# Attention levels of the mixing blocks placed between the streamed projections, S5 directly behind them, products by halves on GpSimd

## The reference, cut to what matters

```python
u, q, k, v, g_out, a_low = jnp.split(h @ w_in[layer], IN_SPLITS, axis=-1)
y_s5 = _s5_group(u, ...)          # 32 groups of 64 complex states, recurrence over the tokens
y_gla = _gla_group(q, k, v, g_out, a_low, w_alpha_up, b_alpha, head_gain)
y = jnp.concatenate([y_s5, y_gla], axis=-1) @ w_out[layer]
```

## Time and profile before

| | us |
|---|---|
| timed runs, median of 3 | 2970.05 |
| the profiled execution | 2976.95 |
| its span, first to last instruction | 2975.2 |
| TensorE busy | 2657.4 |
| VectorE busy | 2241.1 |
| ScalarE busy | 1465.4 |
| GpSimd busy | 941.0 |
| mean granted TensorE clock | 0.925 of full |

### The profile page before, as it was taken

How to read it: one execution, slowest core, us unless ns; L and a number is a source line. 1 busy time by engine, 2 the same in 40 slices (tenths; PEclk the granted TensorE clock), 3 DMA queues, 4 the chain that set the end, 5 groups by cost and what they waited for, 6 DMA issues and landing times. The chain is left out here.

```text
span 2975.2 us, 47277 instructions
## 1 busy us (share of the span) xinstructions
PE 2657.4 (89%) x17674; PEld 2414.6 (81%) x17674; DVE 2241.1 (75%) x2501; ACT 1465.4 (49%) x1886; POOL 941.0 (32%) x568
## 2 busy tenths in 40 slices
PE   7998689999998897568997756799999999999997
PEld 7998489999988887348997633699999999999986
DVE  6676566766767755877777677589888888988888
ACT  4343443433444334114333311477777777777765
POOL 6970059788408301324999142000000000000000
PEclk9999599999999998689998858899999999999999
DMA  8764067677444453025773301499999999999986
GB/s 292 250 209 149 22 226 248 217 248 253 168 186 156 162 176 131 25 68 208 255 241 114 131 22 54 164 344 344 336 346 344 341 345 331 342 343 341 344 311 228
DMA packets 129207, 670.56 MB, mean 225 GB/s; under 512 B 14672, under 2 KB 14992, under 8 KB 80064
## 3 DMA queue, kind: packets, MB, share of 16 engines
q1 hardware_dynamic: 111024, 604.72, 55.6%
q0 software_dynamic: 18064, 64.21, 6.3%
HBM read 667.82 MB, written 1.05 MB: 225 GB/s over the span
## 5 line engine op out<-in xcount | busy, mean ns | idle before, releaser
L1595 PE MATMUL work<-xT_hi,wh_gu 128*128 128x256 f32 x2120 | 611.2, 288 | 57.1 <-DVE xT_lo L871 25.2
L1596 PE MATMUL work<-xT_lo,wh_gu 128*128 128x256 f32 x2120 | 608.7, 287 | 0.0
L1597 PE MATMUL work<-xT_hi,wl_gu 128*128 128x256 f32 x2120 | 608.0, 287 | 0.0
L1595 PE MATMUL work<-wh_gu,mixT_hi 128*128 128x256 f32 x1792 | 513.0, 286 | 4.7 <-DVE mixT_lo L1317 3.2
L1596 PE MATMUL work<-wl_gu,mixT_hi 128*128 128x256 f32 x1792 | 505.7, 282 | 0.0
L1597 PE MATMUL work<-wh_gu,mixT_lo 128*128 128x256 f32 x1792 | 505.4, 282 | 0.0
L754 DVE TENSOR_TENSOR wl_gu<-raw_gu,wh_gu 128x2048 fp32r<-128x2048 f32 x158 | 390.2, 2469 | 124.3 <-ACT wh_gu L378 123.8
L1595 PEld LDWEIGHTS work<-xT_hi,wh_gu 128*128 128x128 f32 x2120 | 415.7, 196 | 68.5 <-issue 39.7
L1596 PEld LDWEIGHTS work<-xT_lo,wh_gu 128*128 128x128 f32 x2120 | 416.4, 196 | 4.8
L1597 PEld LDWEIGHTS work<-xT_hi,wl_gu 128*128 128x128 f32 x2120 | 415.5, 196 | 0.0
L1595 PE MATMUL acc<-wh_d,h_hi 128*128 128x512 f32 x912 | 379.6, 416 | 4.5 <-DVE wl_d L1329 2.7
(11 more groups left out here) (438 smaller groups left out, 4873.8 us busy)
## 6 DMA issues: line engine op xcount, KB each, us to landing
raw_gu<-in_w_gu SPq DMA_DIRECT2D x271, 1024.0 KB, 4.9
raw_d<-in_w_d SPq DMA_DIRECT2D x269, 512.0 KB, 5.4
scratch<-in_w_gu SPq DMA_DIRECT2D x112, 1024.0 KB, 7.2
scratch<-in_w_d SPq DMA_DIRECT2D x112, 512.0 KB, 7.8
scratch<-in_w_mod POOLq DMA_DIRECT2D x96, 512.0 KB, 3.7
scratch<-in_s_b POOLq DMA_DIRECT2D x16, 256.0 KB, 2.9
rows<-in_norm_post POOLq DMA_DIRECT2D x6, 512.0 KB, 4.4
rows<-in_ln_g POOLq DMA_DIRECT2D x4, 512.0 KB, 4.0
```

Source lines behind the costliest of these rows:

```text
L1595: pe.matmul(out_, w[0], m[0], start=start, stop=False)
L1596: pe.matmul(out_, w[0], m[1], start=False, stop=False)
L1597: return pe.matmul(out_, w[1], m[0], start=False, stop=stop)
```

## The change

- TensorE: the alpha product stands behind unit U+1, the identity set behind the first part of U+2, and levels 0 to 7 behind the parts of units U+3 to U+5 (`stream` with `behind`). Behind them come the first S5 product, the products with v, the second S5 product, and the transposes, which now go to the banks 0 and 1 of `work`.
- ScalarE: it evacuates the q, k, alpha, v and u blocks, and applies Silu straight from PSUM.
- VectorE: it makes `CS` behind the low part of U+2, takes the low parts of U+4 to U+6 behind masks 0, 3 and 6, puts each level into `SC` with `copy_predicated` from PSUM instead of a product and a sum, and scales, gains and gates the heads inside round 0 of S5 with one instruction for a head and token tile; the low parts of the heads go into round 1.
- GpSimd: a level multiplies the left half of each pair of stretches with keys and the right half with queries, in place, in the buffer of the decays, which serves as both operands of the scores. It multiplies the gate by the head gain, and loads `CRAW` ahead of the levels.

The core of the diff:

```diff
@@ TensorE, mix2
-                unit(U, [T, T, T])
-                unit(U + 1, [T, T, v[0]])
-                unit(U + 2, v[1:4])
-                unit(U + 3, go[0:3])
-                unit(U + 4, [go[3], T, T])
-                unit(U + 5, [T, None, T])
-                pe.wait_ge(t_evac, TSTART[b + 1])
-                pe.wait_ge(alphaw_in, 16 * (n + 1))
...
+                def level(j):
+
+                    if j < 0:
+                        pair_scores(QG, KG, 0).then_inc(g["scores"], 1)
+                        return
+                    pe.wait_ge(g["decayed"], 8 * n + j + 1)
+                    x = DF[j % 3]
                     if j:
                         pe.wait_ge(g["masked"], 9 * n + j)
-                        pair_scores(QS[j % 2], KS[j % 2], (j + 1) % 2).then_inc(g["scores"], 1)
-                        continue
+                        pair_scores(x, x, (j + 1) % 2).then_inc(g["scores"], 1)
+                        return
+                    pe.wait_ge(g["zabs"], n + 1)
...
+                t_, u_ = [t_block(i) for i in range(5)], [u_block(i) for i in range(4)]
+                stream(U, t_[0:3])
+                stream(U + 1, [t_[3], t_[4], v[0]])
+                alpha()
+                stream(U + 2, v[1:4], (-1, None, None))
+                stream(U + 3, go[0:3], (0, 1, 2))
+                stream(U + 4, [go[3], u_[0], u_[1]], (3, 4, 5))
+                stream(U + 5, [u_[2], None, u_[3]], (6, None, 7))
...
                 bu(0)
+                heads()
                 bu(1)
-                pe.wait_ge(mix_l, MSTART[b] + 2)
+                heads_transposed()
@@ ScalarE, mix2
-                for u in range(6):
-                    hi(U + u + 1)
...
+                hi(U + 1)
+                if b > SECOND:
+                    act.wait_ge(x_done, b)
+                keep(0, QG[:, 0:S], gu_used, U + 1, HD ** -0.5)
+                keep(1, QG[:, S:2 * S], gu_used, U + 1, HD ** -0.5)
+                keep(2, KG[:, 0:S], d_used, U + 1)
+                hi(U + 2)
+                keep(3, KG[:, S:2 * S], gu_used, U + 2)
+                keep(4, AL, gu_used, U + 2)
+                hi(U + 3)
                 act.wait_ge(g["zabs"], n + 1)
...
+                decay(0)
+                decay(1)
+                act.wait_ge(d_used, U + 3)
+                act.activation(VG, PA[:, 0:2, :], ACT.Copy).then_inc(g["vg_sb"], 1)
+                hi(U + 4)
+                decay(2)
+                decay(3)
+                decay(4)
+                hi(U + 5)
+                decay(5)
+                decay(6)
+                keep_u(0, gu_used, U + 5)
+                decay(7)
+                act.wait_ge(gu_used, U + 5)
+                act.activation(GO, PA[:, 2:4, :], ACT.Silu).then_inc(g["gout"], 1)
+                keep_u(1, d_used, U + 5)
+                hi(U + 6)
@@ VectorE, mix2
+                differences(0)
+                differences(1)
+                masked(-1)
+                for j in range(8):
+                    if j + 2 < 8:
+                        differences(j + 2)
+                    masked(j)
+                    if j in (0, 3, 6):
+                        lo(U + 4 + j // 3)
...
-                        link(masked(j - 1, j, (j + 1) % 2))
-                        TT(SC[:, 0:2], SC[:, 0:2], MT.rearrange("p (w h i) -> p w h i", w=2, h=4),
-                           ALU.add).then_inc(g["masked"], 1)
...
+                            here = masks[:, j - 1:j, :].broadcast_to([P, 4, P]).bitcast(I32)
+                            last = dve.copy_predicated(SC[:, w], here, ps)
...
+                    dve.wait_ge(g["root"], n + 1)
+                    link(dve.reciprocal(grs, grs))
+                    dve.wait_ge(g["gained"], n + 1)
+                    for t in range(NT):
+                        for h in range(4):
+                            v = slice(h * P, (h + 1) * P)
+                            last = STT(OG[:, t, v], PB[:, t, v], grs[:, 4 * t + h:4 * t + h + 1], GO[:, t, v],
+                                       ALU.mult, ALU.mult)
@@ GpSimd
+                    pool.wait_ge(xt_l, 4 * (b + 1))
+                    pool.dma_start(CRAW, A["s5_c"][n]).then_inc(s5c_in, 16)
                     for j in range(8):
+                        df = halves(j, DF[j % 3])
                         pool.wait_ge(g["exp"], 8 * n + j + 1)
-                        if j >= 2:
-                            pool.wait_ge(g["scores"], 9 * n + j)
-                        TT(QS[j % 2], DF[j % 3], QG, ALU.mult).then_inc(g["qks"], 1)
-                        TT(KS[j % 2], DF[j % 3], KG, ALU.mult).then_inc(g["qks"], 1)
-                    pool.wait_ge(g["og"], n + 1)
-                    pool.dma_start(CRAW, A["s5_c"][n]).then_inc(s5c_in, 16)
+                        TT(df[:, :, 0, :], df[:, :, 0, :], halves(j, KG)[:, :, 0, :], ALU.mult)
+                        TT(df[:, :, 1, :], df[:, :, 1, :], halves(j, QG)[:, :, 1, :], ALU.mult).then_inc(g["decayed"], 1)
+                    pool.wait_ge(g["gout"], n + 1)
+                    pool.wait_ge(headgain_in, 16 * (n + 1))
+                    TT(GO, GO, HG.unsqueeze(1).broadcast_to([P, NT, 512]), ALU.mult).then_inc(g["gained"], 1)
+                    pool.wait_ge(g["decayed"], 8 * (n + 1))
```

More of the change, by code:

```diff
@@ L189, in program @@
[L189 to L192, removed]
+        DF = [view(5632 + 512 * i, 512) for i in range(3)]
+        LT = DF[2]
+        BT = view(7168, 512)
+        AL, GJ = view(7680, 256), view(7936, 128)
         SC = ROW[:, 0:1536].rearrange("p (w h i) -> p w h i", w=3, h=4)
-        OG = ROW[:, 1536:2560].rearrange("p (t d) -> p t d", t=NT)
+        VG = ROW[:, 1536:2560].rearrange("p (t d) -> p t d", t=NT)
@@ L196, in program @@
         HG = ROW[:, 2560:3072]
+        GO = first_net.rearrange("p (t d) -> p t d", t=NT)
+        OG = view(6656, 1024).rearrange("p (t d) -> p t d", t=NT)
         SBM = [view(1024 + 512 * i, 512).rearrange("p (c t m) -> p c t m", c=2, t=2) for i in range(2)]
[L199 to L202, removed]
@@ L206, in program @@
+        PP = [view(4608 + 512 * i, 512) for i in range(4)]
+        TURNED = [[ROW[:, 512 * i:512 * i + 512] for i in range(4)],
+                  [ROW[:, 2048:2560], HG, first_net[:, 0:512], first_net[:, 512:1024]]]
+        YT = view(6656, 1024).rearrange("p (k s) -> p k s", k=4)
         GL = view(2048, 1024).rearrange("p (k s) -> p k s", k=4)
@@ L1875, in mix2, with stream, then @@
-                pe.wait_ge(g["og"], n + 1)
-                for t in range(NT):
-                    for k in range(4):
-                        last = pe.transpose(PB[:, 2 + t, k * P:(k + 1) * P], OG[:, t, k * P:(k + 1) * P], ident)
-                    last.then_inc(g["oT"], 1)
+                def stream(u, parts, behind=(None, None, None)):
+                    def then(i):
+                        if behind[i] is not None:
+                            level(behind[i])
+                    pe.wait_ge(gu_lo, u + 1)
+                    last = parts[0](u, 0)
+                    if parts[1] is None:
+                        last.then_inc(gu_used, 1)
+                    then(0)
+                    if parts[1] is not None:
+                        parts[1](u, 1).then_inc(gu_used, 1)
+                    then(1)
+                    pe.wait_ge(d_lo, u + 1)
+                    parts[2](u, 2).then_inc(d_used, 1)
+                    then(2)
@@ L1881, in bu, with heads_transposed @@
+                def heads_transposed():
+                    pe.wait_ge(g["og"], n + 1)
+                    for t in range(NT):
+                        for k in range(4):
+                            last = pe.transpose(PB[:, t, k * P:(k + 1) * P], OG[:, t, k * P:(k + 1) * P], ident)
+                        last.then_inc(g["oT"], 1)
                 def bu(r):
```

229 lines of the change are left out of this document (119 added, 110 removed).

## The result

The changed kernel takes 2870.69 us (median of 4 runs, 2868.46 to 2872.15) where the kernel before, timed beside it, takes 2970.08 (4 runs, 2966.34 to 2972.00): a ratio of 0.9666, 95% interval 0.9649 to 0.9683, 99.4 us less. The forecast was 2873. The profiled execution took 2870.16 us (span 2868.4).

What follows compares the result with a forecast made beforehand. Between projections and S5 no engine is full; they hand one level around. Starting S5 52.5 us earlier, less 4.0 us it takes back, gives 48.5 a block: 2970 - 97 = 2873 us, own range 2862 to 2885.

Steps and rivals of the forecast that it cites:

- Order and path on TensorE: Projections and levels: alpha product, eleven parts and the score sets run without a stall, last set ending at 1181.1.
- 11 x 2.75 = 30.2: TensorE in the levels: the eleven remaining projection parts cost what they cost before, 2.75 us each, 30.2 us.
- the walk: Level-by-level count from U+1's end: last set at about 1183, S5's first VectorE product at 1186.8, before any allowance.
- the rival with sets at 2.08 us: Levels run at the low clock: nine sets cost 8.5 us more a block, 2890 us; chance 0.11.
- Predicated copy: VectorE's masks in the levels: two copies replace two products and a sum, 0.64 us each, up to 1.3.
- the rival's condition: VectorE becomes the wall of the levels if a predicated copy takes 1.3 us: 2887 us; chance 0.18.
- the 6 us added to VectorE: Sharing with GpSimd in the levels: 1 us in each of six levels, bringing VectorE from 26 to 32 us.
- The allowance of 2 us: Start of S5: 2 us for unplaced alternations with GpSimd moves its first VectorE product from 1186.8 to 1188.8.
- +4.0 forecast: S5 takes back about 4.0 us a block: fused gating, a reciprocal and the heads' two low parts on VectorE.
- Behind S5: Last S5 step, GELU, gated unit and projection out keep their order; nothing counted, changed stage lengths a sign of error.
- it doesn't overlap: In-order queues of ScalarE and VectorE interlock, so only removed work counts, 21 us a block: 2928 us; chance 0.03.
- the estimate by that rule alone: All sixteen GpSimd products (10 us) push VectorE, 2 us a block more than allowed: 2877 us instead of 2873.

Runs made afterwards that it cites:

- e1: The changed kernel with all nine score sets behind the last projection and the low parts of U+3 to U+6 ahead of the decay chain: 2917.8 us.
- e4: The changed kernel with PSUM product and sum in place of the predicated copies: 2880.28 us.
- e8: The changed kernel with GpSimd issuing the loads of S5's input weights ahead of its gain product: 2871.95 us.
- e6: The changed kernel with VectorE's eight gating instructions in S5's round 0 issued twice: 2876.59 us.
- e9: The changed kernel with ScalarE scaling heads, one VectorE gate product in S5's round 1, and round 2's state inputs ahead of the head transposes on TensorE: 2868.26 us.
- e3: The kernel before with GpSimd multiplying halves in place, nothing else: 2956.38 us.
- e2: The kernel before with each level's mask product and sum replaced by two predicated copies, nothing else: 2957.35 us.
- e10: The kernel before with both the predicated copies and the in-place half products, levels still behind the projections: 2945.42 us.
- e7: The changed kernel with ScalarE scaling the heads and GpSimd multiplying by the gate in S5, both taken off VectorE: 2875.11 us.

## Why the prediction was right

The forecast, 48.5 us a block, was met by 49.7, half of the timed 99.4 (by the two profiles 51.0 and 53.5: the first stage gives 55.3 and 56.1, S5 takes back 3.3 and 3.5). That the time comes within 2.3 us of the forecast is luck in part: the savings were worked out in the profile's times, and in these they are 7.5 us more than the 97 of the forecast, but the profile of before lay 6.9 above its median. The mechanism was as forecast. Its steps:

- *Order and path on TensorE.* "11 x 2.75 = 30.2" stands. The sets were priced at 1.1 us by the start distances of other matmuls in the earlier trace rows; the row is 1.16, and with the change to and from projections a set costs 1.29 to 1.41 of TensorE's time. Over eight and a half sets that is 2 us a block too little. The stalls of 0.9 and 1.0 us for masks 1 and 4 did not occur, 1.9 too much. So the last set ended 42.8 us after U+1's end, the walk had it at 42.6: right by two errors that cancel.
- *The clock.* At 1.00 throughout, so the rival with sets at 2.08 us fell. e1 shows the other side: with 1.4 us idle between sets some run at 1.16 and later ones at 2.08 us, mean clock 0.66.
- *Predicated copy.* 0.64 taken; two take 1.33 to 1.42 us, 0.62 to 0.66 from start to start. Its upper bound of 1.3 was the rival's condition, and that fell; e4 shows that 5.4 to 5.8 us more a block appear once VectorE's load goes up.
- *GpSimd.* 0.62 taken for a half product; 0.73 alone, 0.85 to 1.02 beside VectorE's differences, up to 2.48 beside a low part. The level's slack hid it all. The idea that this side carries the alternation is right, but the 6 us added to VectorE were more than it paid: from the identity mask on (1147.0) it is busy for 29.8 us where 32 were counted, and some 4.6 of these are stretches (differences of 0.42 at 0.94 to 1.06, low parts at 2.43 and 2.60).
- *Start of S5.* The walk ended 46.4 us after U+1's end, the allowance made it 48.4; measured 45.63 and 45.25. The allowance of 2 us for alternations that the walk didn't place was the mis-sized term: there was nothing to place, since VectorE waits 1.1 to 2.6 us for TensorE at three levels and takes stretches up there. Mask 7 ended first and the load decided, by 0.8 us; DMA issue to use was 3.4 us, not 4.0. The prediction named that wait as a sign of being wrong, though its own walk had the two ends as a tie. It came, at 0.8 and 0.4 us, and e8 shows that it costs nothing: without it mask 7 decides.
- *S5.* +4.0 forecast, +3.3 and +3.5 measured; e6 shows that work put there is paid in full, e9 that less work there comes back.
- *Behind S5.* The prediction said that it would be wrong if those stages changed length. They did, by -1.0 to +1.25 us each, in both directions, net 0.1: the stage with the last output step takes 5.37 and 6.61 us in before, 6.62 and 5.76 in after, and 4.09 and 5.74 in the repeat of after, so it varies from run to run of one kernel. The granted clock of the step goes with it: 1.00 for 4.09 us, 0.71 to 0.74 for 5.37 to 5.76, 0.50 to 0.54 for 6.6. That the clock alone does it was not tried by itself.

Of the rivals, "it doesn't overlap" had the removed work at 21 us a block and 2928. The mechanism isn't what happened, but e1 puts a number on it: 2918, 26 a block. The count of removed work was off in both directions. By themselves the half products shorten the first stage by 7.0 and 7.7 us a block (e3) where the count had 3, since they stand in the chain from level to level; the copies give 6.0 and 7.6 (e2) where it had 13 for the sums. And it left out what e1 leaves over e10 (e10 is 14 to 15 us a block shorter in the first stage than before, e1 32). That difference lies nearly whole behind the levels: from the last copy to S5's first product e10 still takes 23.4 and 23.1 us, e1 5.4 and 5.5. Which part of the rearrangement (heads, table, loads) gives how much of it wasn't tried piece by piece.

The Trainium skill (GPSIMD Engine Reference, Key points) has GpSimd contend with VectorE instructions of two SBUF inputs, and the estimate by that rule alone was 2877. The rows agree with the direction of the rule and not with that sum: products were stretched on both engines, on VectorE by 4.6 us a block and not by 10, and neither engine was the one that set the pace.

## What to carry to other kernels

When a stage hands one item around several engines, put it between pieces of work that keep one of them full, and look at what stands behind it in the order as well: what e1 no longer had there was 18 us a block. Count for each engine the load in the merged stage: here TensorE 44.9, VectorE 39.6 of 45.7 us, and seven sums more on VectorE would have cost a tenth of the gain. Work taken off a full engine is only saved if nothing in an in-order queue waits for it: look at what stands behind the waiting instruction (e7's transposes with the next round's inputs behind them), and at what the new engine's accesses stretch.

## What the runs showed of the hardware

- A copy predicated by a broadcast int32 mask, from PSUM to 128x512 of float32 in SBUF, takes 0.70 to 0.78 us, and the second of a pair starts 0.62 to 0.66 us behind the first; products of that shape with one input in PSUM start 0.60 us apart.
- VectorE and GpSimd, each with two SBUF inputs, stretch each other instruction by instruction, and in each of these rows the one that started second is the longer one: 0.42 us become 0.94 to 1.49, four scans of 2.44 become 4.46, a low part of 2.28 becomes 4.18 beside GpSimd's 128x1024 product, and GpSimd's 0.73 becomes 2.48 beside a low part that keeps its 2.28. S5's products with one input in PSUM kept 0.66 to 0.69 us, beside GpSimd's products too.
- One score set of sixteen 64-row matmuls takes 1.16 us at the full granted clock and 2.08 at half, and in a level of 2.6 us either can occur within one stage (e1).
